# Rotary partner rows by DMA instead of a TensorE permutation; the second half of each S5 table turned from the first by ScalarE

## The reference

```python
def partial_rope(x, cos, sin):            # on the first 16 of each 64 dims of q and k
    x1, x2 = xr[..., :half], xr[..., half:]          # half = 8
    rot = concatenate([x1 * c - x2 * s, x1 * s + x2 * c])

for l in range(DEPTH):                    # DEPTH = 2
    h = rmsnorm(x, ln1_g[l])
    proj = h @ w_in[l]                    # 28 units of 128 columns, one for each mixer's part
    q = partial_rope(rmsnorm(q, qk_norm_g[l, 0]), cos, sin)   # 4 heads x 2 x 64
    k = partial_rope(rmsnorm(k, qk_norm_g[l, 1]), cos, sin)
    o_a = diff_attention(q, k, v, ...)    # 512 channels
    o_b = sc_b * causal_dwconv(sc_c * sc_h, ...)
    o_c = s5_mixer(...)                   # 16 groups x 64 complex states: x_t = lam_bar * x_{t-1} + b_bar u_t
    o_d = mamba2_mixer(...)
    x = x + concatenate([o_a, o_b, o_c, o_d]) @ w_out[l]
    x = x + (silu(causal_dwconv(h2 @ gate)) * (h2 @ up)) @ down
```

## Time and profile before

| | us |
|---|---|
| median of 3 runs | 1415.01 (1414.2 to 1416.82) |
| profiled execution | 1416.61 |
| its span | 1414.8 |
| TensorE busy | 1352.1 (96%) |
| VectorE busy | 920.0 (65%) |
| GpSimd busy | 685.4 (48%) |
| ScalarE busy | 500.5 (35%) |

### The profile page before, as it was taken

The page is one execution under the profiler, slowest core; times in us unless marked ns, Lnnn a source line. Parts: engine busy times, 40 slices in busy tenths (PEclk is TensorE's granted clock), DMA queues, the critical chain, the costliest instruction groups (busy, mean ns, idle before and its releaser), DMA issues.

```text
span 1414.8 us, 15816 instructions
## 1 busy us (share of the span) xinstructions
PE 1352.1 (96%) x6116; PEld 1057.2 (75%) x6116; DVE 920.0 (65%) x1225; ACT 500.5 (35%) x751; POOL 685.4 (48%) x368
## 2 busy tenths in 40 slices
PE   2999999799999999999999999989999999999999
PEld 1787666477788888888878775657778888888887
DVE  7769888575777604777227788876567773077730
ACT  4342434565422212223333333445553232123221
POOL 1655788222444443444457468961244444444442
PEclk9999999999999999999999999999999999999999
DMA  5221112012333322333232111110133233223232
GB/s 193 78 87 60 56 49 66 25 45 54 113 102 95 106 97 89 93 101 112 83 118 84 66 48 57 60 60 23 46 97 105 89 111 107 80 90 105 95 108 95
DMA packets 33947, 118.46 MB, mean 84 GB/s; under 512 B 3792, under 2 KB 3920, under 8 KB 33872
## 3 DMA queue, kind: packets, MB, share of 16 engines
q1 hardware_dynamic: 33584, 116.39, 25.9%
q10 hardware_dynamic: 288, 1.05, 0.2%
HBM read 114.28 MB, written 2.10 MB: 82 GB/s over the span
## 4 chain that ended last, share of the span: by engine, by line
PE 89%; DVE 7%; ACT 1%; issue 1%; DMA 1%; POOL 1%; SPq 0%; DVEq 0%; POOLq 0%
PE bank L395 26%; PE bank L397 26%; PE bank L405 26%; PE bank L449 1%; PE bank L595 1%; PE bank L458 1%; PE bank L424 1%; PE bank L554 1%; PE bank L556 1%; PE bank L576 1%; DMA raw<-in_w_first 1%; PE bank L586 1%; DVE xl L966 1%; DVE ml L1000 1%; PE bank L478 0%
## 5 line engine op out<-in xcount | busy, mean ns | idle before, releaser
L295 POOL TENSOR_TENSOR wl<-raw,wh 128x1024 fp32r<-128x1024 f32 (+3 forms) x208 | 500.5, 2407 | 650.4 <-ACT wh L722 408.4
L395 PE MATMUL bank<-xl,wh 128*128 128x512 f32 x1152 | 300.4, 402 | 29.1 <-ACT wh L722 18.1
L722 ACT ACTIVATE wh<-raw 128x1024 fp32r<-128x1024 f32 (+3 forms) x208 | 218.5, 1051 | 240.3 <-PE bank L397 221.6
L395 PEld LDWEIGHTS bank<-xl,wh 128*128 128x128 f32 x1152 | 216.2, 190 | 101.6 <-issue 41.4
L397 PE MATMUL bank<-xh,wh 128*128 128x512 f32 x1152 | 288.0, 392 | 0.0
L405 PE MATMUL bank<-xh,wl 128*128 128x512 f32 x1152 | 286.8, 391 | 0.0
L397 PEld LDWEIGHTS bank<-xh,wh 128*128 128x128 f32 x1152 | 218.4, 190 | 46.0
L405 PEld LDWEIGHTS bank<-xh,wl 128*128 128x128 f32 x1152 | 216.9, 189 | 45.4 <-issue 0.3
L1004 DVE TENSOR_TENSOR x<-x,bank 128x512 f32<-128x512 f32 x64 | 44.0, 688 | 225.1 <-PE bank L405 225.1
L395 PE MATMUL bank<-ml,wh 128*128 128x512 f32 x512 | 133.4, 402 | 0.0
L397 PE MATMUL bank<-mh,wh 128*128 128x512 f32 x512 | 127.8, 390 | 0.0
(11 more groups left out here) (266 smaller groups left out, 1422.0 us busy)
## 6 DMA issues: line engine op xcount, KB each, us to landing
raw<-in_w_gu SPq DMA_DIRECT2D x88, 512.0 KB, 3.5
raw<-in_w_in SPq DMA_DIRECT2D x52, 512.0 KB, 3.5
raw<-in_w_dn SPq DMA_DIRECT2D x32, 704.0 KB, 4.1
raw<-in_w_oe SPq DMA_DIRECT2D x16, 384.0 KB, 3.0
raw<-in_w_ol SPq DMA_DIRECT2D x16, 256.0 KB, 2.7
x<-in_x SPq DMA_DIRECT2D x8, 256.0 KB, 6.4
raw<-in_w_first SPq DMA_DIRECT2D x4, 512.0 KB, 6.7
out_x<-x SPq DMA_DIRECT2D x8, 256.0 KB, 4.5
```

The lines of the kernel that those rows point to most:

```text
L295: tt(wl[:, p, 0:cols], raw[:, p, 0:cols], wh[:, p, 0:cols].bitcast(F32), ALU.subtract).then_inc(wl_full, 1)
L395: mm(bank[b][:, :], wh[:, p, k * P:(k + 1) * P], lo[:, k, :], start=(k == 0), stop=False)
L722: fn(wh[:, p, 0:cols], raw[:, p, 0:cols], ACT.Copy).then_inc(wh_full, 1)
```

## The change

The rows of Q and K are laid out anew by the host, so that each head's 32 rotated rows lie in the middle (rows 48 to 79), the two rows of a rotated pair beside each other. The partner of a row is then one row up or down, and SP fetches all partners with two DMAs of 16 rows (SBUF to SBUF) into a `partner` tile instead of TensorE's product with `permg`. The sign goes into the sine table, the gain of the partner into `partg`. VectorE puts the sine table into bank 5 once a layer; `qk_finish` works in bank 4, after ScalarE has read the sum there.

`table` makes only the first 256 columns. ScalarE makes four scaled copies of them (by the cosine and the sine of 256 theta), and GpSimd's new `table_end` makes the second 256 columns from these with two operations, one step later.

```diff
+HALF = T // 2
+TURN = FINE + HALF // FINE
@@ sync, in the loop over the units g @@
                 if g >= 2:
                     sp.wait_ge(wl_full, g - 1)
+                s = g % (len(UNITS) // L) - 4
+                if 16 <= s < 24:
+                    sp.wait_ge(unit_out, unit_out_of(g // (len(UNITS) // L), s))
+                    for to, of in ((0, 1), (1, 0)):
+                        sp.dma_start(partner[s % 2][ROT0 + to:ROT1:2, :],
+                                     G[ROT0 + of:ROT1:2, s % 2, :]).then_inc(partner_in[s % 2], 16)
                 sp.dma_start(raw[:, g % 2, 0:cols], src[l, i]).then_inc(raw_full[g % 2], 16)
@@ gpsimd, table(l, j): all on [:, 0:HALF] now @@
-                tt(sin, sin, s5t[:, :], ALU.add).then_inc(tab_full, 1)
+                tt(sin, sin, t, ALU.add).then_inc(tab_base, 1)
+
+            def table_end(l, j):
+                cos, sin = [t[:, HALF:T] for t in tab[j % 2]]
+                pool.wait_ge(tab_turned, l * SJ + j + 1)
+                tt(cos, cos, s5t[:, 0:HALF], ALU.subtract)
+                tt(sin, sin, s5t[:, HALF:T], ALU.add).then_inc(tab_full, 1)
                 temp_free.append((tab_full, l * SJ + j + 1))
@@ gpsimd, in the loop over the steps s @@
                     if s in TABLE_AT:
                         table(l, TABLE_AT.index(s))
+                    if s - 1 in TABLE_AT:
+                        table_end(l, TABLE_AT.index(s - 1))
                     if s == 11 or s == 15 or s >= 17 and s % 2:
                         s5_imaginary(l, 0 if s == 11 else (s - 13) // 2)
@@ tensor @@
                 pe.wait_ge(sqk_ready, nth(sqk_ready))
-                claim(4, act_free[4])
+                claim(4, qk_done)
                 mm(bank[4][:, :], block1, G[:, 2, :], start=True, stop=True).then_inc(act_bank[4], 1)
-                claim(5, qk_done)
-                mm(bank[5][:, :], permg[:, t % 2, :], G[:, t % 2, :], start=True, stop=True).then_inc(dve_bank[5], 1)
-            def attend(n):
+            def attend(l, n):
+                if n == 0:
+                    pe.wait_ge(qk_done, 8 * (l + 1))
@@ scalar @@
+                def table_turned(j):
+                    act.wait_ge(tab_base, l * SJ + j + 1)
+                    turn = [rot[:, l, i, j, TURN:TURN + 1] for i in range(2)]
+                    cos, sin = tab[j % 2]
+                    temps = s5t[:, 0:HALF], s5t[:, HALF:T]
+                    for out, of, c in ((cos[:, HALF:T], cos, 0), (temps[0], sin, 1),
+                                       (sin[:, HALF:T], sin, 0), (temps[1], cos, 1)):
+                        w = fn(out, of[:, 0:HALF], ACT.Copy, scale=turn[c])
+                    w.then_inc(tab_turned, 1)
                 for s in range(1, NIN):
                     prep()
+                    if s - 1 in TABLE_AT:
+                        table_turned(TABLE_AT.index(s - 1))
@@ vector @@
                 own(stt(q, G[:, p, :], par_of(l, "qkg", p), cosT, MUL, MUL))
-                dve.wait_ge(dve_bank[5], nth(dve_bank[5]))
-                after(tt(bank[5][:, :], bank[5][:, :], sinT, MUL))
-                after(tt(bank[5][:, :], q, bank[5][:, :], ADD))
+                dve.wait_ge(partner_in[p], 32 * (4 * l + t // 2 + 1))
+                dve.wait_ge(act_free[4], nth(act_free[4]))
+                after(stt(bank[4][:, :], partner[p], par_of(l, "partg", p), bank[5][:, :], MUL, MUL))
+                after(tt(bank[4][:, :], q, bank[4][:, :], ADD))
                 dve.wait_ge(qk_rms, nth(qk_rms))
-                tt(q, bank[5][:, :], G[:, 3 + p, :], MUL).then_inc(qk_done, 1)
+                tt(q, bank[4][:, :], G[:, 3 + p, :], MUL).then_inc(qk_done, 1)
@@ vector, step s == 15, behind s5_back @@
+                        nc.vector.memset(partner[0], 0.0)
+                        nc.vector.memset(partner[1], 0.0)
+                        dve.wait_ge(yz_ready, 2 * (l + 1))
+                        own(copy(bank[5][:, :], sinT))
@@ vector, parameters(l) @@
+                ts(par_of(l, "partg"), par_of(l, "partg"), QK ** -0.5, None, MUL)
-                for i in range(2):
-                    ts(permg[:, i, :], perm, par_of(l, "qkg", i), None, MUL)
...
```

More of the change, by code:

```diff
@@ L20 @@
 ROPE = 16
+ROT0, ROT1 = QK - ROPE, QK + ROPE
 THETA = 500000.0
@@ L45 @@
 CONSTS, _o = {}, 0
-for _name, _n in [("ident", P), ("ones", P), ("tri", P), ("perm", P), ("block", P), ("cap", P), ("eps", 1)]:
+for _name, _n in [("ident", P), ("ones", P), ("tri", P), ("block", P), ("cap", P), ("eps", 1)]:
     CONSTS[_name] = slice(_o, _o + _n)
@@ L51 @@
 PARAMS, _o = {}, 0
-for _name, _n in [("g1", KD), ("g2", KD), ("qkg", 2), ("subg", 1), ("oneml", 1), ("scw", 6),
+for _name, _n in [("g1", KD), ("g2", KD), ("qkg", 2), ("partg", 2), ("subg", 1), ("oneml", 1), ("scw", 6),
                   ("s5d", 2), ("bglu", 2), ("m2w", 24), ("m2b", 6),
@@ L141, in build @@
         rho_all = sb("rho_all", [P, L, SJ])
-        permg = sb("permg", [P, 2, P])
+        partner1 = sb("partner", [P, T], at=offsets["hst"])
+        partner = (G[:, 5, :], partner1[:, :])
         par_all = sb("par_all", [P, L, NPAR])
@@ L154, in build @@
         bank = [ctx.enter_context(nc.psum_tensor(f"bank{b}", [P, T], F32)) for b in range(8)]
-        ident, ones, tri, perm, block1, cap = [
-            cst[:, CONSTS[k]] for k in ("ident", "ones", "tri", "perm", "block", "cap")]
+        ident, ones, tri, block1, cap = [
+            cst[:, CONSTS[k]] for k in ("ident", "ones", "tri", "block", "cap")]
         cosT, sinT = rotary[:, 0, :], rotary[:, 1, :]
@@ L189, in build @@
         yz_ready, m2sq_ready, m2_rms = sem("yz_ready"), sem("m2sq_ready"), sem("m2_rms")
+        tab_base, tab_turned = sem("tab_base"), sem("tab_turned")
         tab_full, tab_free, cf_ready, s5_scanned = sem("tab_full"), sem("tab_free"), sem("cf_ready"), sem("s5_scanned")
@@ L196, in build @@
         em_full, em_high, mixed_ready = sem("em_full"), sem("em_high"), sem("mixed_ready")
+        partner_in = [sem(f"partner_in{p}") for p in range(2)]
         sqk_ready, qk_rms, qk_done, v_ready = [sem(n) for n in ("sqk_ready", "qk_rms", "qk_done", "v_ready")]
@@ L303, in table @@
                     pool.wait_ge(tab_free, l * (SJ - 2) + j - 1)
[L304 to L308, removed]
+                shape = [P, COARSE // 2, FINE]
+                fine, coarse = slice(0, FINE), slice(FINE, FINE + COARSE // 2)
+                cc, sc = [rot[:, l, i, j, coarse].unsqueeze(2).broadcast_to(shape) for i in range(2)]
+                cfn, sfn = [rot[:, l, i, j, fine].unsqueeze(1).broadcast_to(shape) for i in range(2)]
+                cos, sin, t = [t[:, 0:HALF] for t in (*tab[j % 2], s5t)]
+                cos3, sin3, t3 = [t.rearrange("p (a b) -> p a b", a=COARSE // 2) for t in (cos, sin, t)]
                 tt(cos3, cc, cfn, ALU.mult)
@@ L313, in table @@
                 pool.wait_ge(pool_own, owned())
-                own(tt(cos, cos, s5t[:, :], ALU.subtract))
+                own(tt(cos, cos, t, ALU.subtract))
                 tt(sin3, sc, cfn, ALU.mult)
@@ L688, in _ @@
                     if n:
[L689 removed]
+                        attend(l, n - 1)
                     if n > NQ and n % NQ == 2:
                         head_sum(HEAD_BANK[n // NQ - 1])
[L692 removed]
+                attend(l, STEPS - 1)
                 unit(0, KEARLY, early_hi, early_lo, resid)
@@ L1489, in _ @@
                         residual(o, o % 2)
+PAIRS = [d for i in range(ROPE // 2) for d in (i, i + ROPE // 2)]
+PLAIN = list(range(ROPE, QK))
+QK_ROWS = [(0, d) for d in PLAIN + PAIRS] + [(1, d) for d in PAIRS + PLAIN]
 def constants():
@@ L1502, in constants @@
     half = ROPE // 2
[L1503 to L1509, removed]
+    for row, (_, dim) in enumerate(QK_ROWS):
+        if dim < ROPE:
+            cos[row] = np.cos(ang[:, dim % half])
+            sin[row] = np.sin(ang[:, dim % half]) * (-1 if dim < half else 1)
     c[:, CONSTS["block"]] = r[:, None] // QK == r[None, :] // QK
@@ L1529, in layout @@
     for h in range(HEADS):
-        order += [w[:, :, h * P:(h + 1) * P], w[:, :, a + h * P:a + (h + 1) * P]]
+        rows = np.array([h * P + c * QK + d for c, d in QK_ROWS])
+        order += [w[:, :, rows], w[:, :, a + rows]]
     w_in = units(np.concatenate(order + [w[:, :, b:c]], axis=2))
@@ L1549, in layout @@
     put("g2", tiled(inp["ln2_g"]))
-    put("qkg", np.tile(inp["qk_norm_g"], (1, 1, 2)).transpose(0, 2, 1))
+    dims = np.array([d for _, d in QK_ROWS])
+    put("qkg", inp["qk_norm_g"][:, :, dims].transpose(0, 2, 1))
+    partner = np.where(dims < ROPE, (dims + ROPE // 2) % ROPE, dims)
+    put("partg", inp["qk_norm_g"][:, :, partner].transpose(0, 2, 1))
     put("subg", tiled(inp["subln_g"]))
```

2 lines of the change are left out of this document (1 added, 1 removed).

## The result

| | before | after |
|---|---|---|
| median us | 1415.16 (1414.2 to 1416.82, 4 runs) | 1446.61 (1445.17 to 1447.19, 4 runs) |
| ratio, 95% interval | | 1.0219 [1.0206, 1.0232] |
| profiled execution, its span | 1416.61, 1414.8 | 1445.17, 1443.4 |
| GpSimd busy | 685.4 | 661.2 |
| ScalarE busy | 500.5 | 524.8 |

The forecast was 1434.8 us, its own range 1429 to 1445, the wide one 1419 to 1450. The time is in the wide one, 1.6 us above the first and 11.8 us above the forecast: 31.5 us were lost on the medians where 19.8 had been worked out.

A forecast was written before the change was run, and what follows sets the result against it. TensorE was taken to set the pace at 16.86 us a pair; a new ring of waits, 21.0 a pair, adds +1.7 +10.4 -2.2 = +9.9 a layer: 1415.0 + 19.8 = 1434.8 us. Own range 1429 to 1445, wide 1419 to 1450.

The forecast's parts named there:

- the landing: Partner DMAs of the Q and K units: 32 KB land in 2.0 us, 2.6 from low's end with issue.
- the imaginary part: GpSimd's s5_imaginary after table_end: starts 4.1 us after S, the second scan's end in an even step, and takes 3.9.
- rival D: Long ring in the Q and K units: partner rows land in 5.2 us, 24.2 a turn, 1446 to 1456; chance 0.11.
- the ring: Q and K units, scan to scan: copies, table_end, imaginary part, low, partner DMA, VectorE operations, scan wait in turn; 21.0 us a pair.
- C: Short ring in the Q and K units: copies never hold GpSimd's table_end, 17.5 us a turn, 1415 to 1423; chance 0.13.
- E: Q and K units: short ring holds, TensorE at 1.2 GHz is last, 18.8 us a pair, 1425 to 1430; chance 0.05.
- the sum for a layer: Layer 0's changes up to S(18), over three turns and after S(24): +1.7, +10.4 and -2.2, together +9.9 us, doubled.
- The turn: One pair of Q and K units, second scan's end to the next: 21.0 us, three from S(18) to S(24) 63.0.
- Up to S(18): Layer start to the second scan's end in step 18: copies before emits and Ln at s = 17 cost +1.7 us, 187.6.
- After S(24): From step 24's second scan end to the last imaginary part's end: 17.6 us where it was 19.8, so -2.2.
- The first rule weighed: Partner DMAs: a DMA costs about 2.0 us before its bytes count, so landing is 2.0 and the sum unchanged.
- The other rule: VectorE's sine product: two SBUF inputs contend with GpSimd, one from PSUM stays 0.7 us; otherwise each turn is 1.0 longer.

The follow-up runs named there:

- e1: Kernel after, with ScalarE's four table copies from step 14 on made in the table's own step, ahead of s5_copy: 1424.03 us, ratio 1.0059.
- e2: Kernel after, with SP issuing each unit's partner DMAs one unit earlier, behind the weight load of unit s + 3: 1431.76 us, ratio 1.0114.
- e3: Kernel after, with both the four copies ahead of s5_copy and the partner DMAs one unit earlier: 1415.07 us, ratio 0.9994.
- e9: Kernel before, with only both emits of step 17 and their low parts moved behind the first rotary unit's work: 1406.91 us, ratio 0.9941.
- e12: Kernel after with copies ahead, partner early and emits later, plus sine read from SBUF and rotation summed in bank 5: 1406.66 us, ratio 0.9936.

## Why the prediction was right, and where it was short

The mechanism was the one forecast. Of the views named for it: the scans 21.2 to 22.0 us apart (forecast some 21); GpSimd idle 7.0 us before table_end, released by ScalarE's copy; the sine product waiting for the partner in the even steps and not in the odd, though 1.9 us and not 4, since VectorE came to it later; the landing 1.8 us; the imaginary part at S + 4.64 (4.1). By its number alone the time is also in rival D's range (1446 to 1456), but D asked for partner rows that land in 5.2 us, and they landed in 1.8. e1 and e2 took the two halves of the ring away one at a time, e3 both, and the time fell each time, by 22.6, 14.9 and 31.5 us.

Two of the views were off. TensorE was to idle 5 us a pair and idled (64.59 - 56.22) / 3 = 2.8, the rest of its slack going into matmuls at the lower clock. And in odd steps the sine product waits 2.6 us for Ln behind the copies, which the text had as harmless; e2 shows that it closes a ring of its own at 19.4 us.

Two of the rivals were priced from the wrong turn. The text took 16.86 us as the turn before, but the three turns together took 52.64, 17.55 each. So C's ring of 17.5 would have cost nothing in the three turns, not +1.9 us a layer, and E's of 18.8 would have cost +3.8, not +5.8. The forecast itself goes by 52.6 and is not touched.

The sizes, in the order of the sum for a layer (forecast +9.9; measured +12.8 in layer 0, where the first write of x moved from 281.6 to 294.4 us, and +15.8 in layer 1, 28.6 - 12.8):

- The turn: 21.0 forecast, 21.4, 21.2 and 22.0 measured. The copies were mis-sized, 1.77 us from the first to table_end instead of 1.25: they took 0.50 each, 0.40 from start to start, where I had put 0.31 from a copy of another kind, 0.383 long. The imaginary part, low and the three operations were within 0.1. Issue and landing made 2.46 us behind a queue that started 0.02 after low, against 2.6.
- The last turn has 0.6 more: `scaled(24)` stands before its scan and the text left it out. Three turns are 64.6 instead of 63.0, +1.6.
- Up to S(18): 188.67 against 187.6, +1.1. Two things that hold step 17 up are in its timeline, though how the 1.1 us divide between them is not shown: the copies hold the first emit, and so VectorE's low part (3.14 us of waiting), and table_end of step 16's table holds GpSimd.

```profile
167.46 1.97 PE L427 MATMUL bank<-xh,wl 128*128 128x512 f32 x8
...
169.18 1.14 ACT L778 ACTIVATE mh<-xbc 128x512 fp32r<-128x512 f32 x2
169.35 0.72 POOL L338 TENSOR_TENSOR ssum<-ssum,s5h 128x256 f32<-128x256 f32 x1 [2.91 <-ACT s5h L843]
169.83 1.93 DVE L1034 TENSOR_TENSOR ml<-xbc,mh 128x512 fp32r<-128x512 f32 x2 [3.14 <-ACT mh L778]
...
175.70 2.04 PE L576 MATMUL bank<-G,cst 128*128 128x512 f32 x2 [6.27 <-DVE qk L1340]
```

  The same place before, ahead of the 2.34 us of the earlier trace rows:

```profile
168.98 1.98 PE L405 MATMUL bank<-xh,wl 128*128 128x512 f32 x8
170.79 1.02 PE L554 MATMUL bank<-G,cst 128*128 128x512 f32 x2
```

  The mean in bank 4 now waits for qk_done, which before only the permuting matmul did. Here the account of the prediction was wrong, though not its sum: "with them a wait of 2.34 us ... in each layer" was to leave TensorE. It came back as 6.27. Of the 3.93 us more, 1.55 are a later qk_done (175.70 against 174.15), 1.52 a unit that ended earlier (167.46 against 168.98), and the rest, 0.86, the mean, which before filled the start of that time and now stands behind it. The clock of 171.4 to 187 fell from 0.78 to 0.67. e9 shows what that wait, the clock behind it and the emits that caused it were worth before the change: 8.9 us for both layers.
- After S(24): 18.55 us to the end of the last imaginary part (253.26 to 271.81), forecast 17.6, before 19.8: +1.0.
- Together 3.6 more than forecast (1.59 + 1.07 + 0.95), which makes 13.5 at that end (271.81 against 258.29), of which the attention gave back 0.7.
- Layer 1 was taken to repeat layer 0 and lost 3.0 us more: +1.2 before its step 16's scan, and 16.7 by the scan of step 24 (956.65 against 927.17, less the 12.8), where layer 0 had 14.8. One partner issue took 2.0 us there. Why the layers differ by so much is not settled.

The first rule weighed was of the landing. The Trainium skill's page DMA: Bandwidth & Descriptors (section Anatomy of one DMA) gives about 2.0 us, for DMAs issued by GpSimd. The trace is near it for these, issued by SyncE: 1.8 us at the median. It is not one number: in e2's order the eight pairs of one parity are all issued right behind a weight load, and these landed in 3.2 us at the median, the others in 1.8. The other rule: by the Trainium skill's page GPSIMD Engine Reference (section Specifications) VectorE instructions with two SBUF inputs contend with GpSimd. The trace agrees: the sine product with one of its inputs in PSUM stayed at 0.742 to 0.758 us in all 16 executions, while the cosine product with both in SBUF took 2.92 beside GpSimd's low and 0.74 while GpSimd stood idle. And e12, which put the sine into SBUF, made of these 0.75 us a median of 1.79 in the odd steps and 1.11 in the even ones.

## What to carry to other kernels

When engines hand work round in a fixed order, price a new wait by what is queued behind it on its engine, and follow that until you are back where you began: here two edits that cost -2 and +7 us alone cost +31 together, since one's delay stood in the path of the other. Follow it in every direction: when the longest ring was cut (e2), a second one 2 us below it set the pace. An operation that prepares a later step should not stand in front of what this step hands on; moving four copies gave back 22.6 us. And where a wait leaves with the instruction that waited, look who takes over its bank: a wait on a buffer is inherited.

## What was not expected of the hardware

- A ScalarE copy of 256 columns from SBUF to SBUF with a scale from SBUF took 492 to 500 ns and followed the one before by 0.40 us; without a scale and from PSUM it took 383. Two things differ between them, and no run here separates them.
- The cosine product with two SBUF inputs on VectorE took 2.77 to 2.92 us in the kernel after in all six places where it began within 0.13 us of GpSimd's low (2.34 to 2.39 us), and 0.74 where GpSimd stood idle; the earlier trace rows had 1.77.
- SyncE took 0.58 us to issue a weight load behind the pair of partner DMAs and 0.33 us alone (e2's order); a pair of partner DMAs mostly took 1.14 us (once 2.00), and the 32 KB of each landed in 1.8 us at the median. In e2 the eight pairs that are all issued right behind a weight load landed in 3.2.
- Leaving out 16 products (32 records) left TensorE's busy time where it was, 1352.1 before and 1354.1 after: at the lower of the two levels of the clock (1.2 GHz instead of 2.4) eight matmuls took 3.78 us instead of 2.12.
